# A hybrid decoder step on one core: fused front stages, expert rows added back through TensorE, store order changed in the middle of the expert loop

## The reference, cut to what matters

```python
p_a, p_b, p_g = split_cols(rms_norm(x) @ w_in, (1792, 1304, 2048))
y_a = rwkv_branch(p_a)      # token shift, low-rank decays, per-token recurrence of 8 heads with
                            # 64x64 states, group norm; samples start from a stored state
y_b = nsa(p_b)              # compressed (32-token blocks through an MLP), selected and window
                            # attention; samples read 1024 cached rows by a page table
x = x + (sig(g_a) * (y_a @ w_br_a) + sig(g_b) * (y_b @ w_br_b)) @ w_out
# MoE: top 4 of 32 experts
logits = rms_norm(x) @ w_router + b_router
u = h @ w_up[e] + b_up[e]                       # (1024, 2048) per expert
y = (glu * sigmoid(1.702 * glu) * (lin + 1)) @ w_down[e] + b_down[e]   # (1024, 1024) per expert
x = x + sum over the token's 4 experts of top_w * y
y = rms_norm(x)
```

## Time and profile before

| | us |
|---|---|
| median of 3 runs | 2051.24 |
| lowest, highest | 2048.83, 2066.33 |
| profiled execution, own time | 2057.01 |
| its span, first to last instruction | 2055.0 |
| TensorE busy / VectorE busy / ScalarE busy in the span | 1487.5 / 429.2 / 240.4 |

### The profile page before, as it was taken

One profiled execution on the slowest core, in us unless ns is written; L12 is line 12 of the kernel. 1 busy time (PEld: TensorE's weight loads), 2 busy tenths in 40 slices (PEclk: granted clock), 3 DMA queues, 4 the chain that ended last, 5 costly groups with the idle time before them and its releaser, 6 DMA issues. The chain is left out here.

```text
span 2055.0 us, 18960 instructions
## 1 busy us (share of the span) xinstructions
PE 1487.5 (72%) x6908; PEld 780.3 (38%) x6909; DVE 429.2 (21%) x799; ACT 240.4 (12%) x489; POOL 180.0 (9%) x243
## 2 busy tenths in 40 slices
PE   4996388701697857866498878778788787788880
PEld 3885287701565643854332222222222222222220
DVE  1002643274133423021511001011011011011013
ACT  1110211100032211012210000000000000000001
POOL 1000021000004600000000000000000000000000
PEclk9998677855586558578599999999999999999995
DMA  6341000013203320043399999999999999999993
GB/s 244 123 164 32 2 1 1 1 25 133 104 1 103 98 67 23 1 164 99 130 379 416 416 418 416 416 418 416 417 418 416 417 417 415 416 417 415 416 374 124
DMA packets 112432, 486.76 MB, mean 237 GB/s; under 512 B 18999, under 2 KB 26809, under 8 KB 78802
## 3 DMA queue, kind: packets, MB, share of 16 engines
q1 hardware_dynamic: 102834, 454.40, 55.4%
q0 software_dynamic: 9552, 31.73, 4.4%
HBM read 481.39 MB, written 17.25 MB: 243 GB/s over the span
## 5 line engine op out<-in xcount | busy, mean ns | idle before, releaser
L1769 PE MATMUL bank<-ex_ring,ex_xT 128*64 128x512 f32 x2048 | 495.0, 607 | 139.8 <-DMA ex_ring<-in_w_up 138.3
L1769 PEld LDWEIGHTS bank<-ex_ring,ex_xT 128*64 128x64 f32 x2048 | 126.5, 137 | 479.4 <-DMA ex_ring<-in_w_up 322.4
L1787 PE MATMUL bank<-ex_ring,ex_hT 128*64 128x512 f32 x1024 | 247.1, 605 | 47.4 <-DMA ex_ring<-in_w_down 46.7
L1726 DVE TENSOR_SCALAR ex_g<-bank 128x512 f32<-128x512 f32 x32 | 22.1, 691 | 657.7 <-PE bank L1775 657.7
L275 PE MATMUL bank<-hT,w_group 128*128 128x264 f32 (+1 forms) x656 | 148.7, 391 | 13.0 <-DMA w_group<-in_w_in 13.0
L1787 PEld LDWEIGHTS bank<-ex_ring,ex_hT 128*64 128x64 f32 x1024 | 62.5, 136 | 209.2 <-DMA ex_ring<-in_w_down 128.4
L275 PEld LDWEIGHTS bank<-hT,w_group 128*128 128x128 f32 (+1 forms) x656 | 124.8, 191 | 36.5 <-issue 13.8
L1671 POOL DMA_INDIRECT scratch_choice<-ex_y,ex_di x32 | 33.3, 1041 | 674.9 <-ACT ex_y L1701 651.3
L925 POOL DMA_INDIRECT sel_pages<-in_cache_sel_kv,page_rows x64 | 60.8, 951 | 151.1 <-DVE page_rows L958 131.9
L1687 ACT ACTIVATE ex_xT<-bank 128x512 f32<-128x512 f32 x33 | 19.7, 597 | 337.0 <-PE bank L1750 337.0
L1691 ACT ACTIVATE ex_hT<-bank 128x512 f32<-128x512 f32 x32 | 19.1, 597 | 312.8 <-PE bank L1756 312.8
(11 more groups left out here) (442 smaller groups left out, 1617.2 us busy)
## 6 DMA issues: line engine op xcount, KB each, us to landing
ex_ring<-in_w_up SPq DMA_DIRECT2D x256, 1024.0 KB, 20.7
ex_ring<-in_w_down SPq DMA_DIRECT2D x256, 512.0 KB, 20.2
w_group<-in_w_in SPq DMA_DIRECT2D x10, 2048.0 KB, 7.7
win_rows<-in_state_win_kv SPq DMA_DIRECT2D x8, 512.0 KB, 7.6
w_out_sb<-in_w_out SPq DMA_DIRECT2D x1, 4096.0 KB, 21.9
choice_rows<-scratch_choice SPq DMA_DIRECT2D x2, 2048.0 KB, 10.2
out_win_s<-in_state_win_kv POOLq DMA_DIRECT2D x1, 4088.0 KB, 24.7
w_branches<-in_w_br_a SPq DMA_DIRECT2D x1, 2048.0 KB
```

Of the source, the lines that this page charges most:

```text
L1726: nc.vector.tensor_scalar(g[:], banks[0][:], 7.0, None, ALU.min).then_inc(S["g_ready"], 1)
L1769: mm = mmul(banks[n // 2][lo:lo + SLOTS, :], B["xT"][:, k % 4, SLOTS * (k // 4):SLOTS * (k // 4) + SLOTS], B["ring"][:, k, 512 * n:512 * n ...
L1787: mm = mmul(banks[4][SLOTS * n:SLOTS * n + SLOTS, :], B["hT"][:, k % 4, SLOTS * (k // 4):SLOTS * (k // 4) + SLOTS], B["ring"][:, 8 + j, D ...
```

## The change

The diff rewrites most of the kernel; what it does, stage by stage:

1. **project and rwkv_prepare become one block.** Only the 25 tiles of the two branches are multiplied here, in an order that gives the decay inputs first; the low-rank products, the shift and the key norms run between them on VectorE and ScalarE. The 16 gate tiles move to `attend_prompt`. Weights come in groups of 2 tiles (1 MB). The 4 MB copy of the window output moves from the start to `merge`.
2. **rwkv_chunks** works on 16 blocks of 64x64 (4 chunks x 4 pairs of heads), with the two partition halves as separate products; all four chunks go through the five levels together. Between chunks the state goes through one 64x64 product per head.
3. **rwkv_samples and rwkv_norm disappear as blocks.** Their work is cut into pieces that stand between the steps of `compress`, whose sample states lie on 128 partitions in halves; the bias table, the queries and the branch gates' sigmoid are made there too, one small task per half step (`at_half`).
4. **compress** fetches in 8 pieces (two indirect DMAs each); its first layer takes keys and values of one position at a time, 4 products of 265 columns on 64 rows (K=64); transposes are plain products with the identity.
5. **attend_prompt** has the 16 gate tiles between its units; gates are kept as tanh of half the value.
6. **attend_samples** puts 4 samples side by side in 32-column strips; values are 96 products of 128 columns. Branch weights are loaded during it.
7. **merge** adds x by products with twice the identity, and computes router sums and squares in it.
8. **route** loads two experts' down weights besides the first up weights; the normalised rows are made by ScalarE and TensorE, tile by tile, and each tile is stored by a DMA from ScalarE's queue. The semaphores for the biases (`bias_in`) and for the stored rows (`rows_stored`) last into the expert block, which waits for them there.
9. **expert_tiles** is one block with everything to the end. The ring has 16 slots (8 up, 2 x 4 down), with pieces of 2 MB. A slot's row is no longer written to memory: a matrix of token weights (`back`) is made by VectorE, and 6 products per expert (`comb`) give the rows in token order, which VectorE adds to x. Biases are float32, 6 products per expert. From expert 16 on (`LATE`) the order changes: the activation and the down product of an expert follow its own up product at once, instead of one expert later.

The core of 8 and 9 (the front's part of the diff is told above):

```diff
-                    for k in range(8):
-                        sp.dma_start(B["ring"][:, k, :], a["w_up"][0][0, P * k:P * k + P, :]).then_inc(S["ring_in"][k], 16)
-                    for t, (t0, n) in enumerate(TILES):
-                        sp.wait_ge(hg_ok, t + 1)
-                        sp.dma_start(scratch["h"][t0:t0 + n, :], h[0:n, t, :]).then_inc(st_, 16)
-                    sp.wait_ge(st_, 48)
+                    for q in range(4):
+                        sp.dma_start(B["ring"][:, 2 * q:2 * q + 2, :], a["w_up"][0][0, 256 * q:256 * q + 256, :].rearrange("(p c) n -> p c n", c=2)
+                                     ).then_inc(S["ring_in"][2 * q], 16)
...
+                    down(0)
+                    down(1)
...
+                    for i in range(6):
+                        t, n = i // 2, TILES[i // 2][1]
+                        act.wait_ge(htd, i + 1)
+                        nc.scalar.activation(h[0:n, t, 512 * (i % 2):512 * (i % 2) + 512], row_banks[i][0:n, :], ACT.Copy, scale=ss[0:n, t:t + 1]).then_inc(hg_ok, 1)
+                        if i % 2:
+                            t0 = TILES[t][0]
+                            act.wait_ge(hg_ok, i + 1)
+                            act.dma_start(scratch["h"][t0:t0 + n, :], h[0:n, t, :]).then_inc(S["rows_stored"], 16)
...
-                        pool.indirect_dma_start(halves(scratch["choice"]), bass.IndirectOffsetOnAxis(ap=B["di"][:, 0:1], axis=0), B["y"][:], None,
-                                                bounds_check=last_choice, oob_is_err=False).then_inc(S["y_out"], 16)
-                        pool.wait_ge(S["y_out"], 16 * (e + 1))
...
+                    pool.wait_ge(S["rows_stored"], 48)
...
+                    def comb(e, wait, to, read=None):
+                        pe.wait_ge(S["y_ready"], e + 1)
+                        pe.wait_ge(S["back_ready"], e + 1)
+                        if wait:
+                            pe.wait_ge(S["added"], 6 * e)
+                        for i, (t, bank) in enumerate(to):
+                            if bank == 0:
+                                pe.wait_ge(S["u_read"], read)
+                            hs = slice(SLOTS * (i % 2), SLOTS * (i % 2) + SLOTS)
+                            mm = mmul(banks[bank], B["back"][hs, P * t:P * t + P], B["y"][hs, :], start=True, stop=True)
+                            if i % 2:
+                                mm.then_inc(S["comb"], 1)
...
+                    def expert(e, pair, half, more):
+                        up(e, True, 0, True)
+                        comb(e - 1, True, late_banks, e + 1)
+                        if more:
+                            turn_x(e + 1)
+                        turn_h(e)
+                        down(e, pair, half, True, True)
```

and the sequence of stages:

```diff
-        project()
         rwkv()
         clear_semaphores()
-        compress()
         attend()
         clear_semaphores()
-        merge()
         expert_buffers()
         route()
+        bridge.close()
         experts()
-        finish()
-        with nc.Block() as block:
-            @block.sync
-            def _(sp):
-                sp.wait_ge(win_copied, 16)
-                sp.wait_ge(outs.sem, outs.n)
```

More of the change, by code:

```diff
@@ L1344, in _ @@
+                    act.wait_ge(partd, 1)
+                    nc.scalar.activation(part[:, 0, :], banks[2][:, 0:T], ACT.Copy).then_inc(part_a, 1)
                 @block.vector
@@ new lines, in _ @@
+                    comb(LATE - 2, True, late_banks, LATE)
+                    turn_h(LATE - 1)
+                    down(LATE - 1, LATE // 2 - 1, 1, True, True)
+                    def expert(e, pair, half, more):
[5 more added lines that the diff above has]
+                        down(e, pair, half, True, True)
+                    with pe.Fori(LATE // 2, NEXP // 2 - 1) as pair:
+                        for half in range(2):
+                            expert(2 * pair + half, pair, half, True)
@@ L1973, in build @@
-        project()
+                        pe.wait_ge(y_ready, c + 1)
+                        pe.wait_ge(back_ok, c + 1)
+                        for i, (t, bank) in enumerate(sums):
+                            hs = slice(SLOTS * (i % 2), SLOTS * (i % 2) + SLOTS)
+                            mm = mmul(banks[bank], B["back"][hs, P * t:P * t + P], y[hs, :], start=True, stop=True)
+                        mm.then_inc(comb_ok, 1)
+                    pe.wait_ge(S["added"], 6 * NEXP)
+                    each(pe, further)
```

2822 lines of the change are left out of this document (1612 added, 1210 removed).

## The result

The changed kernel takes 1502.96 us (median of 3 runs, 1498.69 to 1504.16) where the kernel before took 2051.24: a ratio of 0.7323, 95% interval 0.7256 to 0.7391. The profiled execution has a span of 1496.9 us and is the fastest of the three.

A forecast was written before the change was run, and what follows sets the result against it. The prediction took the expert weight stream as the loop's bound, with TensorE waiting on chains before it. Front 633, plus 4 and 940 for the stream, gave 1577; tail 21 made 1598 span, forecast 1596 us, range 1535 to 1700.

The forecast's parts named there:

- What bounds the kernel: Whole kernel: the expert weight stream bounds the loop at 412 GB/s; before it TensorE waits for chains, often at reduced clock.
- The sum of the front: Seven stages up to the first gather: 150 + 80 + 103 + 120 + 60 + 75 + 45 = 633 us instead of 1027.
- The range of the front: Seven stages before the expert loop: all good ends 540 us, all bad ends 750, kept at 590 to 700.
- Route: Last stage before the expert loop: 45 us to the first gather, 70 before; 17.6 MB of weights load behind it.
- The stream: Expert weight loads: 385.3 MB left plus 4.3 MB of gathers at 417 GB/s, 939 us; 30.5 us per expert.
- TensorE in the loop: Expert loop: TensorE needs 27.9 to 30.5 us per expert, 28.5 taken, a near tie with the stream's 30.5.
- TensorE becomes the bound: Rival, expert loop: row halves don't pair, an expert takes about 32.5 us, total about 1665; chance 0.18.
- The change of tiling mode: Expert loop: drains TensorE according to the skill, five changes per expert; no price stated, none visible in the trace.
- The tail: After the last byte: 21 us, range 17 to 30, against 46 before; reading back rows and ten additions go.
- Everything overlaps: Rival: chunks and compress at the paired price, attend_prompt near full clock, tail 17 us, total about 1540; chance 0.08.
- The first test of the profile: Profile after: 416 GB/s or more from slice 17 of 40 to the last but one means the forecast is right.
- The second: Profile after: the first expert product at 630 to 650 us means the forecast of the front is right.

The follow-up runs named there:

- d3: Changed kernel with the first expert's up weights and the first two experts' down weights requested at the start of the expert block, none in route: 1523.4 us.
- c1: Changed kernel with the down weights of experts 0 and 1 requested at the start of the expert block instead of in route: 1503.4 us.
- c4: Changed kernel with ScalarE waiting at the end of route for the stored rows and the biases: 1502.6 us.
- b4: Changed kernel with the ring loaded 128 rows at a time as before, in pieces of 1 MB (up) and 0.5 MB (down): 1521.7 us.
- a3: Changed kernel with all six products back to token order reading partitions 0 to 63, so none runs beside its neighbour: 1547.3 us.
- c3: Changed kernel with each group of 16 small chunk products going through the lower partition half first, then the upper, instead of alternating: 1549.4 us.
- a4: Changed kernel with each of the six products back to token order issued twice into the same bank: 1553.5 us.

## Why the forecast was 93 us too high

By its own steps:

- *What bounds the kernel* held. The front was latency and a half clock, the loop is the stream. "The stream can't be made faster" did not hold (431 instead of 417).
- *The sum of the front is the step that failed*: 588 us up to the ring's first load (633 less route's 45), and 513.4 came. Its terms are of two kinds. *What I added to the products* ("a start of 20", "levels at 7, start 13, end 23", barriers, "the rest" of attend_samples) makes 84 to 99 us over the six stages, as far as the sum can be parted; TensorE's idle time up to 513 us is 47. These allowances were taken from a front whose TensorE waited, but the new one is busy 91% of the time. *The products themselves* make 489 to 504, and TensorE was busy for 466. The 25 tiles were right (90.7; 90.1 measured, 400 instructions at L530), the chunk products a little low (55; 60 busy). Too high were attend_prompt above all (118; 104 busy: I had the units at a mix of half and full clock, and it was granted 0.94), project with its small products (124; 116) and merge (72; 67). So of the 75 us some 37 to 52 are waits, and 23 to 38 are products and their clock. With route, all seven stages came out below, by 6 to 20 us each, 81 in all.
- *The range of the front*, "they hardly all go one way, so I keep 590 to 700", failed with it. All went one way, to 552. The two ends were also added up wrongly: the ranges as given, with 75 for merge and 45 for route, make 555 and 760, not 540 and 750.
- *Route* was counted in full (45 us, with 17.6 MB hidden in it). The real sum starts at the ring's first load at 513.4; route's length hardly counts (d3, c1, c4). Both ways of counting give about the same, since 17.6 MB are 42 us at 417 GB/s. (The ring's three first loads are 8.39 + 2 x 4.19 = 16.8 MB; that is 2 us of difference.)
- *The stream*: the period was forecast as 30.5 us and is 29.5. I gave the larger pieces nothing, because the row of before looked like the limit. (It was read as 415 to 418 "from slice 21 on without a break"; slice 21 has 379, and the last two 374 and 124.) It was not the limit: 431 was to be had. Over 31 periods it is 30 us. Run length and size of the loads explain 6 of the 14 GB/s, about 13 of the 30 us (b4's 19 us hold a late start besides), and the rest has no cause that I could show.
- *TensorE in the loop*: 27.9 at the low end, 28.5 taken; where the changed kernel does not wait for the stream, its up products start 27.35 us apart in the early order (602.37 and 629.72) and 27.8 in the late one (1016.96 and 1044.77 in the chain that ended last). The products back to token order pair (2.85), as taken. The rival "TensorE becomes the bound" is what a3 shows, at 1547: unpaired it needs 30.4, not 32.5. In the changed kernel it is so only up to 753 us and from 994 to 1138, and costs nothing there.
- *The change of tiling mode*, at the one place looked at, has no visible price: 16 instructions of 128*64 and then 12 of 64*128 start 3.58 us apart, against 3.54 for 16 at the plain pace of 1.77 per 8.
- *The tail* was forecast as 21 us after the last byte. The stream stops by 1472 us or so, 25 us ahead of the end, within the 17 to 30 given.
- The rival *Everything overlaps* (1540, given 0.08) came nearest. Its conditions held: the chunk products pair, the first layer of compress nearly does (34.3 us for its 256 instructions, 1.07 per step, against 0.9 and 1.8), and attend_prompt is near the full clock. Its tail of 17 us did not, and it had the stream at 417. The time lies 37 us below it as well.
- The first test of the profile named in the prediction, 416 GB/s or more from slice 17 on, holds to the letter. That is luck: a slice is now 37.4 us and no longer 40, and the pace is another. The second, the first expert product at 630 to 650 us, was wrong (the first turned rows at 552.7, the first up product at 555.6), and told at once that the front was the miss.

The sum of it, for the span: 1598 forecast, 1496.9 in the profile, 101 less. 75 lie before the ring's first load (588 forecast, 513.4 measured), and 27 behind it: 983.5 us in place of 1010, the stream 30 shorter and the tail 4 longer. The median of the runs lies 4 us above the profiled execution and the forecast 2 below its own span, so that 93 are left of the 101.

## What to carry to other kernels

When a rewrite fills TensorE's waits, look at how much of each new stage it will be busy, and do not carry the latencies of the old stage over. Here the busy time plus 10% is the front up to 513 us (466 and 513), and single stages lie at 3 to 18%; as a way to forecast this was not tried on another kernel. Find the first load of the bound stream and count from there: what lies before it counts nearly in full (c3 starts 48.3 us later and ends 49.7 later; d3 starts the ring 26.6 later and takes 20 longer), what lies behind it is free as long as the queue does not run dry and TensorE stays under the stream's period (a3 and a4 went over it by about 1 us per expert and paid 44 and 50). Small products in different partition halves run side by side only when they stand next to each other: alternating took 2.85 us where one half took 5.41 (a3), and 0.94 where one half after the other took 1.5 (c3).

## What was not expected of the hardware

Loads onto 64 partitions halve the stream (218 instead of 431 GB/s) though the engines' busy share stays at 1.01. In a queue that never ran dry the unbroken run per partition was worth 3 GB/s between 8 and 16 KB (428 and 431). In c3 the granted clock fell to 0.81 and 0.67 in a stage in which the records show TensorE busy 95% of the time; the same products in alternating order kept 0.98.
